# Diffusion backbone on one core: fewer modulation pieces in the opening, a third of them added up on VectorE in the MLP

## The reference, cut to what matters

```python
for i in range(DEPTH):                                   # DEPTH = 2
    mx = jnp.split(cond_x @ ada_w[i] + ada_b[i], 6, axis=-1)   # latent tokens; ada_w[i]: 1024 x 6144
    mc = jnp.split(cond_c @ ada_w[i] + ada_b[i], 6, axis=-1)   # context tokens
    hx = modulate(rms_norm(x, g[0]), mx[0], mx[1])             # h * (1 + scale) + shift
    hc = modulate(rms_norm(ctx, g[0]), mc[0], mc[1])
    # i == 0: attention mixer of hx, hc; i == 1: long convolution and SSD
    x = x + mx[2] * rms_norm(ox, g[1])
    x = x + mx[5] * rms_norm(sq_relu_mlp(modulate(rms_norm(x, g[2]), mx[3], mx[4]), ff_w1[i], ff_w2[i]), g[3])
    # the same for ctx with mc, in layer 0 only
```

## Time and profile before

| | |
|---|---|
| profiled execution | 3457.7 us, and its span 3457.7 us |
| median of three runs | 3455.98 us (3452.26 to 3457.7) |
| PE (matmul) busy | 3317.7 us, 96% |
| DVE, ACT, POOL busy | 53%, 37%, 20% |
| moved by DMA | 406.62 MB, mean 118 GB/s |
| stage 1 | from 0 to about 81 us, stage 2 from 82.0 us to about 232 us |
| `ada_ring` loads | 24 of 2048 KB, median 9.8 us from issue to landing |

### The profile page before, as it was taken

One profiled execution on the slowest core, in us unless ns is written; L12 is line 12 of the kernel. 1 busy time (PEld: TensorE's weight loads), 2 busy tenths in 40 slices (PEclk: granted clock), 3 DMA queues, 4 the chain that ended last, 5 costly groups with the idle time before them and its releaser, 6 DMA issues. The chain is left out here.

```text
span 3457.7 us, 39533 instructions
## 1 busy us (share of the span) xinstructions
PE 3317.7 (96%) x15472; PEld 2443.2 (71%) x15472; DVE 1818.6 (53%) x2304; ACT 1291.3 (37%) x2118; POOL 691.5 (20%) x383
## 2 busy tenths in 40 slices
PE   6999999999999999999999999898999999999998
PEld 3666444555788888888889878652456788888886
DVE  3233544433555544554586444588576654445444
ACT  4333344445553333333454223452113532233332
POOL 0000478667331101300120100110011320002001
PEclk8999999999999999999999999999999999999999
DMA  8753533321253333433465311102513333333333
GB/s 329 290 214 103 179 65 77 77 61 48 98 171 127 112 97 97 146 98 96 131 195 175 113 62 39 51 1 101 203 49 109 132 126 97 98 98 117 121 98 104
DMA packets 134552, 406.62 MB, mean 118 GB/s; under 512 B 24153, under 2 KB 38265, under 8 KB 130016
## 3 DMA queue, kind: packets, MB, share of 16 engines
q1 hardware_dynamic: 134368, 404.11, 36.1%
HBM read 345.05 MB, written 58.92 MB: 117 GB/s over the span
## 5 line engine op out<-in xcount | busy, mean ns | idle before, releaser
L1598 PE MATMUL psum<-hid_high,w_high_and_low 128*128 128x512 f32 (+1 forms) x1536 | 416.3, 356 | 11.7 <-DVE hid_low L1831 9.4
L1581 PE MATMUL psum<-h_high,w_high_and_low 128*128 128x512 f32 (+1 forms) x1536 | 415.6, 356 | 0.7 <-DVE w_high_and_low L1741 0.7
L1648 ACT ACTIVATE w_high_and_low<-w_raw 128x1024 fp32r<-128x1024 f32 x226 | 238.6, 1056 | 342.3 <-PE psum L1598 238.8
L1853 POOL TENSOR_TENSOR squares_then_rstd_of_out<-squares_then_rstd_of_out,square_out 128x512 f32<-128x512 f32 (+1 forms) x69 | 103.2, 1495 | 1277.1 <-ACT square_out L1663 1277.1
L1741 DVE TENSOR_TENSOR w_high_and_low<-w_raw,w_high_and_low 128x1024 fp32r<-128x1024 f32 x226 | 285.7, 1265 | 90.9 <-ACT w_high_and_low L1648 90.2
L1313 POOL TENSOR_TENSOR probs_added<-probs_added,probs_turned 128x1024 f32<-128x1024 f32 x128 | 308.1, 2407 | 66.6 <-ACT probs_turned L1238 54.0
L1598 PEld LDWEIGHTS psum<-hid_high,w_high_and_low 128*128 128x128 f32 x1536 | 274.2, 190 | 54.5 <-DVE hid_low L1831 7.8
L1581 PEld LDWEIGHTS psum<-h_high,w_high_and_low 128*128 128x128 f32 x1536 | 273.1, 189 | 42.5 <-DVE w_high_and_low L1741 1.3
L1280 DVE TENSOR_REDUCE row_max<-psum 128x1 f32<-128x1280 f32 x120 | 179.0, 1492 | 228.5 <-PE psum L1176 137.2
L1828 DVE TENSOR_TENSOR hid_high<-hid_relu_and_square 128x512 fp32r<-128x512 f32 (+1 forms) x160 | 111.5, 697 | 351.3 <-ACT hid_relu_and_square L1731 351.2
L1598 PE MATMUL psum<-hid_low,w_high_and_low 128*128 128x512 f32 (+1 forms) x768 | 272.2, 354 | 0.0
(11 more groups left out here) (472 smaller groups left out, 6713.0 us busy)
## 6 DMA issues: line engine op xcount, KB each, us to landing
w_raw<-in_ff_w_dram SPq DMA_DIRECT2D x320, 512.0 KB, 3.6
ada_ring<-in_ada_w_dram SPq DMA_DIRECT2D x24, 2048.0 KB, 9.8
w_raw<-in_w_out_dram SPq DMA_DIRECT2D x38, 512.0 KB, 3.5
scratch_spectra<-spectrum_out SPq DMA_DIRECT2D x32, 256.0 KB, 2.0
filter_ring<-scratch_spectra SPq DMA_DIRECT2D x16, 512.0 KB, 3.9
stream_in<-scratch_x SPq DMA_DIRECT2D x27, 256.0 KB, 4.4
w_raw<-in_w_hy_dram SPq DMA_DIRECT2D x12, 512.0 KB, 3.9
scratch_hyena<-mixed SPq DMA_DIRECT2D x12, 512.0 KB, 2.6
```

Of the source, the lines that this page charges most:

```text
L1581: mm = pe.matmul(bank[:, 0:n], x[i % SLOTS][:, k, :], y[:, k, a:a + n], start=(k == 0 and m == 0), stop=(k == KT - 1 and m == 2))
L1598: mm = pe.matmul(bank[:, 0:n], x[i % SLOTS][:, 2 * k + half, :], y[:, k, 0:n], start=(k == 0 and m == 0), stop=(k == HT - 1 and m == 2))
L1648: act.activation(w_hi[i % SLOTS], raw[i % 2], ACT.Copy).then_inc(w_rounded, 1)
L1853: pool.tensor_tensor(acc_out[:, q % 2, 0:n], acc_out[:, q % 2, 0:n], sq_out[:, v % 2, 0:n], ALU.add).then_inc(added_out, 1)
```

## The change

- **Which piece goes where.** `ADA_FIRST` keeps four pieces (scale A and shift A of layer 0); `ADA_LATER` has the eight others of layer 0, in steps 4 to 11 of stage 2 (`ADA_FROM = 4`); the twelve of layer 1 go into layer 0's `out_and_mlp` as `ADA_IN_MLP`, four batches.
- **How layer 1's are made (`ModulationRows`).** A piece is loaded as eight granules of 256 KB (one K tile each) through two slots. DVE multiplies a granule by the conditioning's scalar of each partition and adds it to a running total (128 instructions of 128x512, two in each of 64 steps of the table `calm`, 32 to a batch). Then PE adds the four totals of a batch over partitions (four matmuls with 32 columns of ones, in column tiles), ACT copies, PE turns (four matmuls of 4 columns), DVE adds bias and gain. `calm` leaves out the steps beside which norms are placed, the last of every eight, and all steps of c2. The first two batches (scale A, shift A) are for both kinds of token: a granule serves two instructions. The last two are for latent tokens alone: two granules a step. Each batch takes one PSUM bank as a unit of its own (`"ada"`).
- **The opening.** SP loads piece 1, then chunks c1 and c2 of x, piece 2, the two weight pieces, piece 3. x is scaled in place, so there is no ring of scaled tiles; the ring of squares has eight slots. All three chunks are squared and scaled ahead of any shift; shifts go in two halves of four K tiles (FRONT needs pieces 0 and 2, BACK pieces 1 and 3). ACT and DVE round and split both weight pieces here. PE makes the first three units of the projection here (`first_unit`, (tile 0, c0), (tile 1, c0), (tile 0, c1)), into banks 0 to 2.
- **Stage 2** has the units in another order (0,c0) (1,c0) (0,c1) (0,c2) (1,c1) (1,c2) and then as before; its PE makes products from unit 3 on (`FIRST = 3`).

```diff
-ADA_FIRST = [(0, piece) for piece in (2, 3, 0, 1, 4, 5, 6, 7, 8, 9)]
-ADA_LATER = [(0, piece) for piece in (10, 11)] + [(1, piece) for piece in range(ADA_PIECES)]
+ADA_FIRST = [(0, piece) for piece in (2, 3, 0, 1)]
+BOTH, LATENT = (0, 1), (0,)
+ADA_LATER = [(0, piece) for piece in range(4, ADA_PIECES)]
+ADA_IN_MLP = [(1, (2, 3), BOTH), (1, (0, 1), BOTH)] + [(1, (4, 5, 6, 7), LATENT), (1, (8, 9, 10, 11), LATENT)]
+class ModulationRows:
...
+    def load(self, sp, m):
+        b, piece, k = self.granules[m]
+        if m >= self.slots:
+            sp.wait_ge(self.stepped, self.rows_by[m - self.slots])
+        sp.dma_start(self.w[:, m % self.slots, :], self.src[self.batches[b][0] * ADA_PIECES + piece][:, k, :]).then_inc(self.w_in[m % self.slots], 16)
+    def add(self, dve, r):
...
+            dve.scalar_tensor_tensor(out=total, in0=w, scalar=scale, in1=total, op0=ALU.mult, op1=ALU.add).then_inc(self.stepped, 1)
+    def add_up(self, pe, b, bank):
+        pe.wait_ge(self.stepped, self.batch_rows[b])
+        for x in range(4):
+            mm = pe.matmul(bank[32 * x:32 * x + 32, :], self.g.ones[:, 0:32], self.total[:, x, :], start=True, stop=True, tile_position=(0, 32 * x))
+    def turn(self, pe, b, bank):
+        pe.wait_ge(self.copied, b + 1)
+        for m in range(BANK // P):
+            mm = pe.matmul(bank[:, 4 * m:4 * m + 4], self.sums[:, m * P:(m + 1) * P], self.g.ident[:, 0:P:32], start=True, stop=True)
...
# opening, SP
-                for i in range(1, NEEDED):
-                    ada.load(sp, i)
+                ada.load(sp, 1)
                 load_x(1)
                 load_x(2)
-                for i in range(NEEDED, A):
-                    ada.load(sp, i)
+                ada.load(sp, 2)
                 for t in range(2):
                     sp.dma_start(g.first_raw[:, t], d["w_qk"][t]).then_inc(w_first, 16)
+                ada.load(sp, 3)
# opening, PE
+                first_unit(0)
+                first_unit(1)
+                first_unit(2)
# opening, ACT
+                act.wait_ge(ada.biased, 3)
+                shift(0, FRONT)
+                shift(1, FRONT)
+                act.wait_ge(w_first, 32)
+                for t in range(2):
+                    act.activation(g.first_high[:, t], g.first_raw[:, t], ACT.Copy).then_inc(w_rounded, 1)
+                ada.copy(act, 3)
+                act.wait_ge(ada.biased, 4)
+                shift(0, BACK)
+                shift(1, BACK)
                 shift(2, range(KT))
# project_attention
-    units = [(t, a, n) for t in range(TILES) for a, n in CHUNKS]
+    TILES, FIRST, ADA_FROM = 5, 3, 4
+    units = [(0, *c0), (1, *c0), (0, *c1), (0, *c2), (1, *c1), (1, *c2)] + [(t, a, n) for t in range(2, TILES) for a, n in CHUNKS]
-                    ada.turn(pe, step - 1)
-                    ada.multiply(pe, step)
+                    ada.turn(pe, step - ADA_FROM - 1)
+                    if step >= ADA_FROM:
+                        ada.multiply(pe, step - ADA_FROM)
# out_and_mlp
+    norm_beside = [(0, 3), (KT + 1, KT + 5), (26, 35), (46, 55), (88, 96), (99, 108), (152, 300), (16, 24)]
+    calm = [i for i in range(N) if not any(a <= i < b for a, b in norm_beside) and (steps[i][1] is None or steps[i][2] != HT - 1)]
...
                     split_weights(i + 2)
+                    for r in rows_at.get(i, ()):
+                        ada.add(dve, r)
```

266 lines of the change are left out of this document (184 added, 82 removed).

## The result

| | before | changed |
|---|---|---|
| median | 3454.12 us (3451.38 to 3457.7, four runs) | 3431.28 us (3430.27 to 3436.09, four runs) |
| profiled execution | span 3457.7 | 3431.53, span 3429.7 |
| PE / DVE / ACT busy | 3317.7 / 1818.6 / 1291.3 | 3292.9 / 1898.4 / 1285.1 |

The ratio is 0.9934, 95% interval [0.992, 0.9948]: faster by 18 to 28 us. A repeat of the changed kernel on another occasion gave 3429.09 beside 3454.38, ratio 0.9924 [0.9911, 0.9936]. The forecast, 3425.5, was 5.8 us too low for the first and 3.6 for the second; both lie in its range. Faster was given 0.94.

A forecast was written before the change was run, and what follows sets the result against it. PE bounds the loop and MLP, bytes and a chain of small steps the opening. 28.1 + 10.4 - 8.0 = 30.5 us less, from 3455.98 to 3425.5 us, range 3414 to 3440.

The forecast's parts named there:

- The opening's walk: Opening up to stage 2: step-by-step times, unit 0 at 53.7, stage 2 starting at 73.6 instead of 82.00 us.
- ACT and clock: Rival, opening: ACT's one queue and half clock set it, gain only 17.5 us, 3438.5; chance 0.13 (the lesser gain).
- The start of stage 2: Stage 2's start: PE waits for the sine table until 81.0; half-swap at 84.9 instead of 113.00, 28.1 us earlier.
- After the mark: Stage 2 behind the half-swap (the mark before unit 3's product): smaller unit, fewer pieces, less half clock; 10.4 us less.
- term (c): Stage 2 behind the half-swap: half clock after the new pause slows the swap and the 256-unit, plus 2.5 us.
- The MLP: Layer 0's MLP: four batches of eight PE matmuls, 1.86 us each, cost 8.0 us, within 7.4 to 11.1.
- DVE at nothing: MLP: DVE's 128 added instructions cost PE 0, up to 0.2 us a step if DVE comes late.
- Slot pace: Rival, MLP: two granule slots set the pace, deciding at load time L = 5.4; 3442 to 3464; chance 0.05.
- no use: Rival: the opening's savings were already hidden and new waits return the rest; 5 us gained, 3451; chance 0.04.
- doesn't do what it says: Rival, opening: six pieces less were hidden behind the norm, waits of 7 and 8 us return the rest; 3451; 0.04.

The follow-up runs named there:

- experiment 3: Changed kernel with ACT rounding the two weight pieces before any shift in the opening, piece 3's copy between FRONT shifts; 3424.0 us, ratio 0.9906.
- experiment 8: Changed kernel with x's last 256 tokens still loaded early but squared, summed and scaled behind unit 0; 3428.03 us, ratio 0.9919.
- experiment 9: Changed kernel with bank, ACT-order and early-table edits, plus squares of the last 256 tokens in PE's gap before piece 3's copy; 3410.55 us, ratio 0.9865.
- experiment 4: Changed kernel with stage 2's four rotation tables loaded at the end of the opening's queue, ring of squares cut to 2; 3423.03 us, ratio 0.9902.
- experiment 2: Kernel before, with only its late w_dt unit put two earlier in the list, giving it bank 0 instead of 2; 3463.83 us, ratio 1.0015.
- Experiments 1: Changed kernel with the late w_dt unit one earlier in the list, giving it bank 5 instead of 0; 3425.78 us, ratio 0.9911.

## Why the prediction was right or wrong

- **The opening's walk** held. Squares of c1 at 27.11 (27.5), shifts at 44.31 (44.7), unit 0 at 53.47 (53.7), stage 2 at 73.6 (73.6). That ACT's one queue sets it, the base of the rival "ACT and clock", is shown by experiment 3; the rival's price did not come: c2's squares ran at full clock (3.72), and only unit 0 at half (5.6 us of it, by 0.85 in 18.70). Piece 3, walked to land near 41, landed at 42.6, where experiments 8 and 9 have PE waiting for it (until 42.67); in the changed kernel nothing waits for it.
- **The start of stage 2** was the right wait, shown by experiment 4. Its size was 1.6 us short in the first trace and right in the repeat.
- **After the mark** 10.4 were forecast. From the half-swap to the mean behind unit 14 13.4 came in the first trace and 11.3 in the repeat. The difference of 2.1 is the clock: term (c), 2.5 us at half clock behind the second pause, was hardly paid in the first trace and was in the repeat. The mark and what is behind it together are 39.3 and 39.1 against 38.5; 1.2 us less is left at the end of the attention. That it met 38.5 so closely in the first trace is partly luck.
- **The MLP** was forecast at 8.0 within 7.4 to 11.1. The batches cost 2.18 each, 8.7, against 1.86 taken: 1.09 for L230 instead of 0.91, the rest at L242 and the slower first products behind it. With the late split in the output projection's steps (next point) it is 10.4 to 11.0. That the lead fell by 5.8 only has another cause: c2's part of the MLP, where nothing of the change runs, lasts 205.1 us in the trace of before, with 13.0 of waiting, and 200.6 in the changed kernel's, with 8.9; twelve other traces have 198.8 to 202.5 there, and 8.4 to 12.3 of waiting. The kernel before with its bank moved (experiment 2) was 3.3 us ahead of it from the stage's start to the MLP's end. So the trace of before was slow there, by chance, and it flatters the change by some 3 us. Why the waits of that part scatter was not tried.
- **DVE at nothing** was right for the MLP's steps, PE 400.00 of 400.00 with and without the instructions, and wrong for the output projection's. There they put a split back, and PE waits 1.65 us for it: 1.7 us on the trace of before, 2.1 to 2.3 on the kernel without them. The forecast had looked at an "up" step alone.
- **Slot pace** did not come: L was 3.6, and the rival's point was 5.4.
- **What failed** is the sentence on what comes behind: I counted PE's eight matmuls per batch and said of the bank that each batch takes "as a unit of its own" nothing at all. The step missing from the sum is the renumbering of the PSUM ring, 5.4 us in layer 1's first product: 2.7 of wait and 2.4 to 2.7 of half clock. Experiments 1 and 2 show it from both sides. Without it the kernel takes 3425.78, the forecast's number. That it meets it to 0.3 us is luck: the MLP's price was 2.4 to 3.0 us too small, and the four runs of that kernel spread over 9 us.
- **The chances** don't quite fit together: "no use" at 3451 has 0.04 and lies within 7 us of before, which as a whole got 0.02.
- The rival "doesn't do what it says" fell: the kernel leads by 38.1 us at the end of the attention although it pays the two waits of 6.58 and 9.82 us, of which experiments 3, 4 and 9 got back most.
- In the changed kernel the part on x's last 256 tokens carries nothing of the gain where its squares and scales are concerned (experiment 8); what its early load is worth was not tried. The squares pay only when placed where PE waits anyway (experiment 9, 2.4 to 2.7 us at the start of stage 2).

## What to carry to other kernels

When a list that numbers a ring of buffers grows by a few entries, work out anew which buffer each later, hand-placed user gets, across the stage's end too: four small units cost 5.4 us in a stage that they don't touch. When a change takes work from the front of a stage, name what that work had covered; here it was a table load and a copy in one engine's queue, and each could be moved for 4 to 6 us. When an engine looks half idle, look at its busiest steps and not at the mean: two more instructions a step in DVE's queue cost nothing in the MLP's steps and 1.7 to 2.3 us in all in the output projection's, beside a norm. A piece of work that doesn't depend on order is free only in a gap: ahead of it or behind it the same squares cost what they take.
